# First layer of a four-layer trunk: loads in order of need, square sums by halves, and a new table of modulation products

## What is computed

```python
m = jax.nn.silu(cond) @ w + b                    # w: 1024 x 6144, cond: two vectors
sh1, sc1, gt1, sh2, sc2, gt2 = split(m, 6)
h = rms_norm(x, g) * (1 + sc1) + sh1             # rms_norm: a mean of squares over 1024
q, k, v = split(h @ w_qkv, 3)                    # then rotary, scores, softmax, P V, sub-norm
x = x + gt1 * (o @ w_o)
```

## Time and profile before

| | us |
|---|---|
| median of 3 timed runs | 2442.58 (2442.09 to 2444.91) |
| the profiled execution | 2447.18 |
| its span on the core | 2445.4 |
| PE busy | 2405.9 |
| DVE, POOL, ACT busy | 1316.7, 1107.1, 1001.8 |
| first product on the values' weights | 20.74 |
| scores of the first layer's tiles 1, 2, 5 and 7 start | 112.98, 133.49, 200.11, 246.05 |

### The profile page before, as it was taken

How to read it: one execution, slowest core, us unless ns; L and a number is a source line. 1 busy time by engine, 2 the same in 40 slices (tenths; PEclk the granted TensorE clock), 3 DMA queues, 4 the chain that set the end, 5 groups by cost and what they waited for, 6 DMA issues and landing times.

```text
span 2445.4 us, 37489 instructions
## 1 busy us (share of the span) xinstructions
PE 2405.9 (98%) x12338; PEld 1983.0 (81%) x12338; DVE 1316.7 (54%) x2347; ACT 1001.8 (41%) x2023; POOL 1107.1 (45%) x839
## 2 busy tenths in 40 slices
PE   9999999999999999999999999999999999999998
PEld 4566788888888888888888887778888888778998
DVE  8997876647253334346664243655766524475321
ACT  3565442232243434433323234664323324466553
POOL 0432444445444344435445434223544543435896
PEclk9999999999999999999999999999999999999999
DMA  8362445556232222235555324222565532323654
GB/s 343 114 112 102 134 159 206 195 173 224 87 100 86 73 73 86 86 104 206 197 182 193 116 79 113 80 84 95 206 206 195 183 111 80 101 78 116 185 181 129
DMA packets 120869, 340.62 MB, mean 139 GB/s; under 512 B 35537, under 2 KB 41937, under 8 KB 120145
## 3 DMA queue, kind: packets, MB, share of 16 engines
q1 hardware_dynamic: 112754, 333.97, 41.8%
q10 hardware_dynamic: 8032, 5.52, 1.6%
HBM read 334.76 MB, written 4.69 MB: 139 GB/s over the span
## 4 chain that ended last, share of the span: by engine, by line
PE 50%; issue 31%; POOL 12%; DVE 4%; ACT 2%; DMA 1%; POOLq 0%; DVEq 0%; ACTq 0%; SPq 0%
PE low_banks L627 39%; POOL w_lo L620 12%; PE high_banks L627 10%; DVE h_lo L1964 1%; DVE tmp L1945 1%; DVE ssum_rstd L1801 0%; ACT w_hi L1276 0%; ACT e_x L1439 0%; DMA xT<-in_xT 0%; DVE rot L2139 0%; DMA ada_raw<-in_ada_w 0%; ACT lnm L1300 0%; DVE ssum_rstd L1933 0%; POOLq L619 0%; DMA w_raw<-in_weights 0%
## 5 line engine op out<-in xcount | busy, mean ns | idle before, releaser
L620 POOL TENSOR_TENSOR w_lo<-w_raw,w_hi 128x512 fp32r<-128x512 f32 x832 | 1106.7, 1357 | 1319.3 <-ACT w_hi L1276 1318.6
L627 PE MATMUL low_banks<-h_hi,w_hi 128*128 128x512 f32 (+2 forms) x1792 | 639.4, 357 | 5.0 <-POOL w_lo L620 1.8
L1276 ACT ACTIVATE w_hi<-w_raw 128x512 fp32r<-128x512 f32 x832 | 473.9, 624 | 395.4 <-PE low_banks L627 192.4
L627 PE MATMUL low_banks<-h_lo,w_hi 128*128 128x512 f32 (+2 forms) x1792 | 632.2, 353 | 0.0
L627 PE MATMUL low_banks<-h_hi,w_lo 128*128 128x512 f32 (+2 forms) x1792 | 630.6, 353 | 0.0
L1801 DVE SCALAR_TENSOR_TENSOR ssum_rstd<-ada_raw,high_banks 128x1024 f32<-128x1024 f32 x304 | 370.7, 1220 | 42.8 <-DMA ada_raw<-in_ada_w 33.9
L627 PEld LDWEIGHTS low_banks<-h_hi,w_hi 128*128 128x128 f32 x1792 | 337.9, 189 | 60.9 <-issue 4.8
L627 PEld LDWEIGHTS low_banks<-h_lo,w_hi 128*128 128x128 f32 x1792 | 338.1, 189 | 46.3 <-issue 1.0
L627 PEld LDWEIGHTS low_banks<-h_hi,w_lo 128*128 128x128 f32 x1792 | 337.1, 189 | 46.6
L1709 ACT ACTIVATE lnm<-low_banks 128x512 f32<-128x512 f32 x66 | 39.4, 597 | 378.2 <-PE low_banks L627 378.2
L2462 DVE TENSOR_TENSOR tmp<-low_banks,lnm 128x512 f32<-128x512 f32 x66 | 45.6, 692 | 211.3 <-ACT lnm L1709 207.6
(11 more groups left out here) (279 smaller groups left out, 3803.6 us busy)
## 6 DMA issues: line engine op xcount, KB each, us to landing
w_raw<-in_weights SPq DMA_DIRECT2D x424, 512.0 KB, 3.7
ada_raw<-in_ada_w SPq DMA_DIRECT2D x152, 512.0 KB, 3.8
ada_first<-in_ada_w SPq DMA_DIRECT2D x24, 512.0 KB, 9.1
v_all<-in_ada_w SPq DMA_DIRECT2D x10, 512.0 KB, 5.5
bias<-rpb_skew SPq DMA_DIRECT2D x64, 64.0 KB, 2.4
rpb_skew<-rpb_rows ACTq DMA_DIRECT2D x1, 3556.0 KB, 34.0
ada_rest<-in_ada_w SPq DMA_DIRECT2D x6, 512.0 KB, 14.0
cond_l<-in_cond SPq DMA_DIRECT2D x3, 1024.0 KB
```

Of the source, the lines that this page charges most:

```text
L620: nc.gpsimd.tensor_tensor(out=w_lo[:, r, part], in0=w_raw[:, r, part], in1=w_hi[:, r, part], op=ALU.subtract).then_inc(lo_ready, 1)
L627: return nc.tensor.matmul(dst, lhsT, rhs, start=start, stop=stop, **kw)
L1276: nc.scalar.activation(w_hi[:, r, part], w_raw[:, r, part], ACT.Copy).then_inc(hi_ready, 1)
```

## The change

It touches the first layer only, but for the name of one semaphore in the last. (1) x comes in three parts (tiles 0 to 3, 4 and 5, 6 and 7); shift chunk 0, biases, gains and scale chunk 8 are loaded between the second and the third, and unit 1 ahead of unit 0. (2) ACT squares tiles 2 to 7, each into its own room, and applies the second SiLU between tiles 5 and 6; DVE squares only tiles 0 and 1. The load of `da_rope` goes behind the roots, since its place holds squares. (3) PE sums all tiles of the latent half, then all of the context half; the three warm-up matmuls are gone. (4) The products of the first pair run c = 0 for both chunks, then c = 1. (5) New tables for chunks 16 to 39: eleven load groups in place of nine, sums four chunks at a time, and in tiles 2 to 5 three products between query and key and none behind the key.

```diff
-WARM = 3
+X_PARTS = ((0, 4), (4, 6), (6, 8))
-ADA_GROUPS = ((16, 0, (16, 17, 0, 4, 1, 5)), (22, 1, (2, 6, 3, 7)), (26, 0, (3,)), (27, 1, (7, 20, 21)),
-              (30, 0, (3, 7)), (32, 1, (20, 21, 22)), (35, 0, (20, 23)), (37, 1, (21, 22)), (39, 0, (20,)))
+ADA_GROUPS = ((16, 0, (16, 17, 0, 1, 5, 2)), (22, 1, (6, 3)), (24, 0, (7, 20)), (26, 1, (21, 3)), (28, 0, (7, 20)),
+              (30, 1, (21, 3)), (32, 0, (22, 20)), (34, 1, (21,)), (35, 0, (22, 23)), (37, 1, (20, 21)), (39, 0, (22,)))
-ADA_VALUES = 4
-ADA_TILE = ((0, 1, 2), (1, 1, 1), (1, 1, 2), (1, 1, 2), (1, 1, 2), (1, 1, 2), (1, 1, 2), (1, 1, 2))
-ADA_TAIL = (1, 9)
+ADA_VALUES = 3
+ADA_TILE = ((0, 1, 1), (0, 0, 2), (1, 3, 0), (1, 3, 0), (1, 3, 0), (1, 3, 0), (1, 3, 1), (1, 3, 1))
+ADA_TAIL = (1, 10)
...
-            for i in range(2):
-                sp.dma_start(xT[:, 4 * i:4 * i + 4, :], xT_in[:, 4 * i:4 * i + 4, :]).then_inc(x_loaded[i], 16)
-                if i == 0:
+            for i, (a, b) in enumerate(X_PARTS):
+                if i == 2:
+                    ada_chunk(0, 0).then_inc(shift_loaded, 16)
                     sp.dma_start(bias_ada[:, :, :], ada_b).then_inc(pair_loaded[0], 16)
                     sp.dma_start(gain[:, :, :, :], gains).then_inc(pair_loaded[0], 16)
-            ada_pair(0)
+                    ada_chunk(KT, 1).then_inc(pair_loaded[0], 16)
+                sp.dma_start(xT[:, a:b, :], xT_in[:, a:b, :]).then_inc(x_loaded[i], 16)
+            loads(1)
             loads(0)
-            loads(1)
...
-            sp.wait_ge(ada_done, 33)
             sp.wait_ge(plan[0].vst_ready, KT)
-            ada_rest_load(6)
+            sp.wait_ge(ada_done, 34)
+            ada_rest_load(8)

             sp.wait_ge(ada_done, 35)
-            ada_rest_load(7)
-
-            sp.wait_ge(ada_done, 36)
-            ada_rest_load(8)
+            ada_rest_load(9)
+
+            sp.wait_ge(ada_done, 37)
+            ada_rest_load(10)
...
-                for i in range(WARM):
-                    mm(bank[7][:, 0:P], ones[:, :], ones[:, :], True, True)
...
+                pe.wait_ge(ssum_step[0], KT)
+                for c, tiles in ((0, range(3, KT)), (1, range(3, KT))):
+                    for m in tiles:
+                        if m > 3 and c == 0:
+                            pe.wait_ge(sq_ready[0], m + 1)
+                        last = summed(m, c)
...
+            act.sem_inc(sq_ready[0], 2)
+            first_silu(0)
+            act.wait_ge(x_loaded[0], 16)
+            first_square(2)
+            first_square(3)
             act.wait_ge(x_loaded[1], 16)
...
+            first_square(4)
+            first_square(5)
+            first_silu(1)
+            log_exp_tables()
+            act.wait_ge(x_loaded[2], 16)
+            act.wait_ge(ssum_step[0], KT)
+            first_square(6)
+            first_square(7)
...
-                        if row == LOOPED - 1 or a == a0 + len(slots) - 1:
-                            ada_sums(a - row, a - row, row + 1)
+                        if row == LOOPED - 1:
+                            ada_sums(a - row, a - row, LOOPED)
...
-                for m in range(1, KT // 2):
-                    own(V.tensor_tensor(out=part[m % 2], in0=xT[:, m, :], in1=xT[:, m, :], op=ALU.mult))
-                    last = V.tensor_tensor(out=ssum[:, :], in0=ssum[:, :], in1=part[m % 2], op=ALU.add)
...
+                own(V.tensor_tensor(out=lnm[:, :], in0=xT[:, 1, :], in1=xT[:, 1, :], op=ALU.mult))
+                own(V.tensor_tensor(out=ssum[:, :], in0=ssum[:, :], in1=lnm[:, :], op=ALU.add))
+                for m in (2, 3):
+                    dve.wait_ge(sq_ready[0], m + 1)
+                    last = V.tensor_tensor(out=ssum[:, :], in0=ssum[:, :], in1=square_room[m], op=ALU.add)
```

More of the change, by code:

```diff
@@ L372, in trunk @@
         small_in, table_in = sem("small_in"), sem("table_in")
-        x_loaded = [sem(f"x_loaded{i}") for i in range(2)]
+        x_loaded = [sem(f"x_loaded{i}") for i in range(3)]
         hi_ready, lo_ready, unit_used = sem("hi_ready"), sem("lo_ready"), sem("unit_used")
@@ L788, in first_square_sum, with summed @@
                     last.then_inc(cond_spread, 1)
[L789 to L796 removed]
+                def summed(m, c):
+                    src = ssum[:, COLS[c]] if m == 3 else square_room[m][:, COLS[c]]
+                    return mm(bank[MS_BANKS[0][c]][:, COLS[c]], ones[:, :], src, m == 3, m == KT - 1)
+                pe.wait_ge(ssum_step[0], KT)
[4 more added lines that the diff above has]
+                        last = summed(m, c)
                         if m == KT - 1:
                             last.then_inc(ms_done[c], 1)
[L799 to L801 removed]
             def values(L, q):
@@ L1732, in ffn, with first_square, first_silu @@
                         nc.scalar.activation(xT[:, m, SEQ:TOK], xT[:, m, 0:SEQ], ACT.Copy, scale=gain_f[:, m:m + 1])
-            for c in range(2):
+            def first_square(m):
+                nc.scalar.activation(square_room[m], xT[:, m, :], ACT.Square).then_inc(sq_ready[0], 1)
+            def first_silu(c):
                 act.wait_ge(cond_spread, c + 1)
@@ L1753, in _ @@
             root(0, 1)
+            act.dma_start(da_rope[:, :, :], da_rope_in).then_inc(table_in, 16)
             for L in plan:
@@ L1811, in ada_sums, with opening_pair, first_pair @@
                                     op=ALU.add))
-            def first_pair(m, between=None):
+            def opening_pair():
+                for c in range(2):
+                    dve.wait_ge(cond_ready, c + 1)
+                    for j in range(2):
+                        if c == 0:
+                            if j == 0:
+                                dve.wait_ge(shift_loaded, 16)
+                            else:
+                                dve.wait_ge(pair_loaded[0], 48)
+                        last = V.scalar_tensor_tensor(out=quarters(dump_0[:, :]), in0=ada_slot(j), scalar=1.0,
+                                                      in1=quarters(cond_0[:, c, :]), op0=ALU.mult, op1=ALU.mult,
+                                                      accum_out=ada_sum[:, j, c:c + 1])
+                        if c == 0:
+                            own(last)
+                        else:
+                            last.then_inc(ada_done, 1)
+                            dve.wait_ge(ada_done, j + 1)
+                modulated(0)
+            def first_pair(m, between):
                 for j in range(2):
                     if j == 0:
-                        dve.wait_ge(pair_loaded[ADA_PAIRS[m]], 32 * ADA_PAIRS.count(ADA_PAIRS[m]) if m else 64)
+                        dve.wait_ge(pair_loaded[ADA_PAIRS[m]], 32 * ADA_PAIRS.count(ADA_PAIRS[m]))
                     for c in range(2):
-                        if m == 0 and j == 0:
-                            dve.wait_ge(cond_ready, c + 1)
                         last = V.scalar_tensor_tensor(out=quarters(dump_0[:, :]), in0=ada_slot(2 * m + j), scalar=1.0,
@@ L2103, in first_values @@
                 for m in range(KT - 1):
-                    first_pair(m, lambda: low_parts(m - 1))
+                    if m:
+                        first_pair(m, lambda: low_parts(m - 1))
+                    else:
+                        opening_pair()
                     for c in range(2):
```

61 lines of the change are left out of this document (27 added, 34 removed).

## The result

The changed kernel takes **2447.9 us** (median of 19 runs, 2443.59 to 2450.84) against 2442.93 for the kernel before (19 runs beside it): a ratio of 1.0019, 95% interval 1.0013 to 1.0025. The forecast was 2443.9 with a range up to 2448.8. The time lies in the range, 4.0 us above the forecast. The interval excludes 1, so the changed kernel is slower, by 0.13 to 0.25%; by the prediction's own line of 0.2% it lies at the slow edge of "the same".

What follows compares the result with a forecast made beforehand. PE, busy 98% of the span, bounds the kernel, so only its waits or low clock count. The terms -1.8 - 3.7 + 5.2 + 2.8 - 1.15 = +1.3 on 2442.58 gave 2443.9 us, range 2436.0 to 2448.8.

Steps and rivals of the forecast that it cites:

- the prediction's own line of 0.2%: Whole kernel: about 0.2%, or 4.9 us, is what a measurement can tell from no change.
- Opening: Start up to PE's first product: second scaling at 18.4 against 20.23, -1.8 us, with ends of -2.4 and -0.5.
- The rival of the missing warm-up: Opening: without warm-up matmuls both rows of sums may stay at 1.2 GHz; opening -0.5, total 2445.2 us; chance 10%.
- Tiles 0 and 1: First layer's attention: fewer products behind values and key bring kT and S1 3.7 us earlier, the opening's part apart.
- S1: S with a number is the start of that tile's scores on PE in the first layer.
- Tiles 2 to 7: Six periods, S1 to S7: late key makes them 133.35 against 133.07 us; +0.3 with low clock in it, +5.2 without.
- Tail: First layer behind the last weights: DVE waits for chunk 35, last sub-norm at S7+28.7, +2.8 us.
- Projection: Behind the tail: one addition of sums less, which took 1.13 us beside POOL, -1.15 us.
- The low clock: PE at 1.2 GHz behind S5 before the change, 4.92 us; forecast sees full clock all through afterwards.
- slower, the low clock comes for waits of the new kind: Around tile 1 and after: PE's new waits bring 1.2 GHz once, 4.92 us, total 2448.8 us; chance 12%.
- The base: Starting time 2442.58 us, the median before, taken as a typical timed run without the low-clock stretch.
- the median had it too: Rival on the starting time: the median had the low clock and loses it, 2439.0 us; chance 20%.

Runs made afterwards that it cites:

- experiment 9: The kernel of experiment 8 with the opening of the kernel before: 2436.25 us, against 2434.67 beside it.
- experiment 1: The changed kernel once more, unedited, a single profiled execution: 2444.16 us.
- Experiment 3: The changed kernel, but in tiles 2 to 5 one product between query and key and two behind the key: 2438.59 us, ratio to before 0.9983.
- experiment 6: The changed kernel (new opening, load groups and sums rule) with the old numbers of products in every place: 2438.62 us, ratio 0.9985.
- Experiment 4: The changed kernel, but chunks 35 and 36 are loaded one chunk earlier, when chunk 32 is done: 2444.38 us.
- experiment 8: The changed kernel with one product ahead of the key in tiles 2 to 5, two in 6 and 7, and earlier tail loads: 2434.55 us, again 2434.67.
- 10: The changed kernel with the three warm-up matmuls put back ahead of the sums, a single execution: 2444.98 us.
- experiment 5: The new opening alone, with the chunk tables, load groups and sums rule of the kernel before: 2442.75 us, ratio 0.9997.

## Why the prediction came out as it did

**Opening: right.** Predicted -1.8, with ends of -2.4 and -0.5. The first product moved from 20.74 to 18.77, the second scaling from 20.23 to 18.12. DVE has summed its tiles by 9.85, and ACT's squares of tiles 6 and 7 and the second half's sums fell where they were put:

```profile
12.25 0.63 ACT L1747 ACTIVATE ssum_rstd<-xT 128x512 f32<-128x512 f32 x1
12.79 0.61 ACT L1747 ACTIVATE lnm<-xT 128x512 f32<-128x512 f32 x1
...
14.80 0.60 PE L637 MATMUL high_banks<-ssum_rstd,ones 128*128 128x256 f32 x2
...
18.12 0.48 DVE L1989 SCALAR_TENSOR_TENSOR tmp<-xT,amp,ssum_rstd 128x256 f32<-128x256 f32 x1 [1.53 <-ACT ssum_rstd L1311]
```

By timed runs it is 1.6 (experiment 9). With old opening the first product came at 20.42, 20.74 and 21.18, with the new one in eleven profiles between 17.78 and 19.35: a spread of 1.6 us that comes mostly from the moment at which the sums change from 1.06 to 0.60 us a row, between about 13 and 16. The rival of the missing warm-up is refuted: the pace rose in no profile later than in the two of the kernel before, with or without it. The Trainium skill (TensorE: Matmul & The Clock Gate, Part 1: The HAM clock gate) says that the number of slow matmuls at a start is run-variable, which these profiles bear out; that fewer matmuls ahead would leave both rows slow, as I had drawn from its rule, they do not.

**Tiles 0 and 1: right.** -3.7 predicted. S1 came 5.87 earlier, of which 1.97 is the opening: -3.9. The wait for a_z is 0.70 as said.

**Tiles 2 to 7: right without the low clock.** 133.35 predicted, 133.37 measured in experiment 1. That the sum agrees to 0.02 is luck: the first period was 22.94 and not 23.25, and the other five took 0.02 to 0.11 more each than forecast. Experiment 3 shows that the three products ahead of the key are the cause. A link of the chain in tile 3, to be laid beside the earlier trace rows: from recip to kT it is now 12.5 us, of which 3.8 are products.

```profile
166.38 0.20 DVE L2221 RECIPROCAL d_st<-d_st 128x8 f32<-128x8 f32 x1
...
172.45 1.22 DVE L1918 SCALAR_TENSOR_TENSOR dump<-ada_first,cond 128x1024 f32<-128x1024 f32 x1
...
178.47 0.42 DVE L2190 TENSOR_TENSOR kT<-high_banks,rot 128x256 f32<-128x256 f32 x1
```

What was right by luck of method: I compared from S to S and so had the 5 us of the old groups' load wait in the 133.07 without knowing it. I called that stretch "idle stretches of PE before S5" and did not ask who caused them. DVE's waits in the kernel before have it, and experiment 6 shows that the new groups remove it, and with it the low clock that the earlier trace rows show:

```profile
188.73 1.23 DVE L1874 SCALAR_TENSOR_TENSOR dump<-ada_first,cond 128x1024 f32<-128x1024 f32 x1 [4.79 <-DMA v_all<-in_ada_w]
```

**Tail: right.** Sub-norm at S7+28.73 (28.7 predicted), one wait for v_all of 3.46 (3.4), landing 5.9 behind the release. Experiment 4 takes it away.

**Projection: the term of -1.15 was not earned.** One addition of sums less is there, but the amplitudes behind it, 0.16 us before, now fall beside POOL, which makes four low parts from 289.27 there and not two from 289.98:

```profile
288.21 1.13 DVE L1830 TENSOR_TENSOR mod<-ada_sum,bias_ada 128x8 f32<-128x8 f32 x1
...
294.46 1.26 DVE L1934 SCALAR_TENSOR_TENSOR amp<-mod,gain 128x16 f32<-128x16 f32 x1
```

1.13 saved, 1.10 given back. Experiments 8 and 9, the same tables with the new and the old opening, have POOL at work beside this instruction in the one and done 0.47 us ahead of it in the other:

```profile
272.73 8.63 POOL L633 TENSOR_TENSOR w_lo<-w_raw,w_hi 128x512 fp32r<-128x512 f32 x5
280.14 1.25 DVE L1937 SCALAR_TENSOR_TENSOR amp<-mod,gain 128x16 f32<-128x16 f32 x1
```

```profile
276.00 6.93 POOL L631 TENSOR_TENSOR w_lo<-w_raw,w_hi 128x512 fp32r<-128x512 f32 x4
283.40 0.16 DVE L1901 SCALAR_TENSOR_TENSOR amp<-mod,gain 128x16 f32<-128x16 f32 x1
```

So it is in all fourteen profiles: 0.16 in the four where POOL is done, 1.25 or 1.26 in the ten where it is not. With this term at nothing, tail and projection are +2.8 and not +1.65; the bookkeeping below has +2.4 to +2.55.

**The low clock: the step that failed.** The sum set it at nothing and the rival "slower, the low clock comes for waits of the new kind" at 12%. It cost 4.8, 4.7, 1.6 and 0 us in the four profiles that have the wait of 2.4 us before S2 (the changed kernel, experiments 4, 10 and 1), and the median of 19 runs is 3.7 above the execution without it. The argument for the 12% was that two waits of 1.9 and 2.2 us before S1 had brought no fall. That was one sample of something that is drawn anew in each execution. A wait of 2.25 us before S1 brought no fall in any of four profiles with the old numbers, one of 2.37 before S2 did in three of four; waits of 1.2 to 1.9, one per tile, never did. Chance has its part in the tail too: behind its wait for y_lo the clock fell after 2.01, 2.38, 3.17, 3.32, 3.40 and 3.53 us and did not after 1.78, 2.25 and 3.15. There DVE sets the pace, and in the five such falls with the new opening the first layer ended 0 to 0.7 us later. So the steps' sum, +1.3, is the time of an execution that is spared, 2444.16, and the rival's 2448.8 is that of the typical one, 2447.9. That the two meet so closely is in part luck, since the projection's term was missed and the base is open (below). What differs between the place before S1 and that before S2, other than the 0.1 us, is open.

**The base: half settled.** I took the typical timed run of before to be without the low clock. Both its profiles and that of experiment 5 have it (4.8, 3.2 and 1.6 us), so "the median had it too" is partly true. Take each profile's own stretch off and it is 2442.4 and 2442.85, near the median of 2442.9, but the lowest timed run is 2440.07, and the first product alone varies by 0.8. How often the timed runs have the stretch can't be said from their times; it stays open.

The bookkeeping of the profiled execution: opening -1.97, tiles 0 and 1 -3.90, S1 to S7 +5.07 (138.14 against 133.07, low clock in both), from S7 to the end +1.60 (2200.95 against 2199.35): +0.8, which is the difference of the spans. The +1.60 looks like the forecast's +2.8 - 1.15, but it is not. DVE's first step behind the root of the feed-forward layer's norm stands in the kernel before, in the changed kernel and in experiment 1 at

```profile
298.66 0.27 DVE L1939 MEMSET ssum_rstd<- 128x256 f32 x1 [1.84 <-ACT ssum_rstd L1301]
```

```profile
300.41 0.27 DVE L1983 MEMSET ssum_rstd<- 128x256 f32 x1 [1.84 <-ACT ssum_rstd L1311]
```

```profile
295.52 0.27 DVE L1983 MEMSET ssum_rstd<- 128x256 f32 x1 [1.83 <-ACT ssum_rstd L1311]
```

That is S7+52.61, S7+55.16 and S7+55.03: the tail and the projection cost +2.55 and +2.42. The other -0.95 of the changed kernel's profile lies in what follows, which the change does not touch: it takes 2145.8 to 2146.1 us in four of the fourteen profiles and 2146.7 to 2146.9 in the other ten, and what decides that is open.

## What to carry to other kernels

Work spread over a steady loop has to be judged link by link: the chain of DVE had 0.6 us of room at the key, and each product ahead of it beyond that cost its full 1.26 us (the period up to S6 is 20.5 with one product ahead, 21.27 with two in experiment 8, 22.53 with three in experiment 3, the tile before the same), while the same product behind the key cost nothing as long as the sub-norm behind it was in time. A late operand costs more than the wait if the matrix engine idles for it: price such a stretch, 2.4 us here, at the wait plus up to 4.8 us, and look in several profiles, since one that shows full clock proves nothing. And where a load wait appears, ask first whether its buffer was free earlier than its release: here one changed number in the loader's waits was worth 3.5 us.

## What the runs showed of the hardware

A single idle stretch of 2.37 us of PE was enough for the granted clock to fall from 2.4 to 1.2 GHz in three of four profiles, and over the seven profiles with such a stretch before S2 or S5 the loss was 0, 1.6, 3.2 or 4.7 to 4.8 us. The shortest wait behind which it fell was 2.01 us (tail of experiment 6), the longest behind which it did not was 3.15 us (tail of experiment 1). With the 1.36 us of filler matmuls the idle part of the wait before S2 was 0.97 and the clock held. The Trainium skill (TensorE: Matmul & The Clock Gate, HAM oscillation — how this bites in real kernels) tells the same mechanism for waits on loads, where PE falls back and the next piece of work starts slow. Here the wait is for another engine, and the trace agrees in kind; the waits of the page's example are 3 to 5 us, those here were enough at 2.0 to 2.4. The kernel of experiment 8 was not only faster but steadier: its ten runs spread over 1.3 us, against 6 to 7 for 19 or more runs of the kernel before and the changed one. That the missing stretch is the reason is likely but not shown: experiments 3 and 6, without one in the tiles but with one in the tail, spread over 5.1 and 5.8 us, and experiment 9, with one in the tail, over 0.6.
